# A weight unit's low part on GpSimd: four instructions of 256 columns instead of one of 1024

## What is computed

```
mem_n = rmsnorm(mem)                                  # 256 memory rows
for l in 0, 1:
    x += rmsnorm(even_mixer(x) if l == 0 else odd_mixer(x))
    x += rmsnorm(memory_cross_attention(x, mem_n @ w_mem_kv[l]))
    x += rmsnorm(relu(h @ w_ff1[l]) ** 2 @ w_ff2[l])  # 4096 wide
x = second block: conv + RWKV-7 mixer, then PEER:
    q = h2 @ peer_wq; top-16 of 128 keys twice; top-16 of the pairs
    out = sum over experts of gelu(h2 . peer_u[e]) * gate * peer_v[e]   # 16384 experts
```

## Time and profile before

| | |
|---|---|
| median of 3 runs | 3501.17 us (3498.74 to 3503.02) |
| the profiled execution | 3501.14 us |
| its span | 3499.9 us |
| PE busy | 3248.4 us (93%) |
| DVE busy | 2253.0 us (64%) |
| POOL busy | 1715.9 us (49%), of which L462 1363.0 us |
| ACT busy | 1358.3 us (39%) |
| mean granted PE clock | 0.967 |

### The profile page before, as it was taken

One profiled execution on the slowest core, in us unless ns is written; L12 is line 12 of the kernel. 1 busy time (PEld: TensorE's weight loads), 2 busy tenths in 40 slices (PEclk: granted clock), 3 DMA queues, 4 the chain that ended last, 5 costly groups with the idle time before them and its releaser, 6 DMA issues.

```text
span 3499.9 us, 48015 instructions
## 1 busy us (share of the span) xinstructions
PE 3248.4 (93%) x18529; PEld 2740.7 (78%) x18529; DVE 2253.0 (64%) x3780; ACT 1358.3 (39%) x2196; POOL 1715.9 (49%) x931
## 2 busy tenths in 40 slices
PE   6997888999899888999898898999999998999997
PEld 6886677888776677888576755799999998788886
DVE  4176646555544556553566646276998995888888
ACT  4444434222344434222253314333333674333332
POOL 6742323444332323444242202447888544888885
PEclk9998999999999999999898899999999999999999
DMA  5520212444322212443220011338899899999995
GB/s 193 183 76 25 87 58 92 137 139 139 108 91 67 84 45 88 145 144 109 69 85 31 3 37 60 120 141 292 295 325 326 266 311 304 372 357 350 354 356 219
DMA packets 304819, 584.76 MB, mean 167 GB/s; under 512 B 13520, under 2 KB 224464, under 8 KB 287312
## 3 DMA queue, kind: packets, MB, share of 16 engines
q1 hardware_dynamic: 252512, 373.32, 31.5%
q0 software_dynamic: 42576, 153.83, 12.2%
q10 hardware_dynamic: 9504, 54.53, 4.1%
HBM read 522.91 MB, written 58.72 MB: 166 GB/s over the span
## 4 chain that ended last, share of the span: by engine, by line
PE 64%; POOL 13%; DVE 9%; issue 8%; ACT 3%; DMA 1%; POOLq 0%; DVEq 0%; SPq 0%; ACTq 0%
PE bank L476 14%; PE bank L478 14%; PE bank L477 14%; POOL split_low L462 9%; PE twin L476 3%; PE twin L478 3%; PE twin L477 3%; PE bank L2854 2%; PE bank L557 2%; PE bank L2279 2%; POOL rows_arena L3220 2%; DVE branch L598 1%; POOL rows_h L3220 1%; POOL rows_near L3220 1%; DVE residual L648 1%
## 5 line engine op out<-in xcount | busy, mean ns | idle before, releaser
L462 POOL TENSOR_TENSOR split_low<-weights,split_high 128x1024 fp32r<-128x1024 f32 x554 | 1363.0, 2466 | 1494.7 <-ACT split_high L454 1490.9
L476 PE MATMUL bank<-normed_high,split_high 128*128 128x512 f32 (+1 forms) x2024 | 748.0, 370 | 34.6 <-issue 25.9
L477 PE MATMUL bank<-normed_low,split_high 128*128 128x512 f32 (+1 forms) x2024 | 736.7, 364 | 0.0
L478 PE MATMUL bank<-normed_high,split_low 128*128 128x512 f32 (+1 forms) x2024 | 736.5, 364 | 0.0
L454 ACT CAST split_high<-weights 128x1024 fp32r<-128x1024 f32 x554 | 571.4, 1046 | 359.8 <-PE bank L478 202.0
L476 PEld LDWEIGHTS bank<-normed_high,split_high 128*128 128x128 f32 x2024 | 384.1, 190 | 84.2 <-issue 37.0
L477 PEld LDWEIGHTS bank<-normed_low,split_high 128*128 128x128 f32 x2024 | 384.1, 190 | 41.6 <-issue 2.7
L478 PEld LDWEIGHTS bank<-normed_high,split_low 128*128 128x128 f32 x2024 | 383.3, 189 | 41.1
L476 PE MATMUL bank<-split_high,wide_hidden_high 128*128 128x512 f32 x768 | 300.2, 391 | 12.6 <-DVE wide_hidden_low L3076 7.4
L478 PE MATMUL bank<-split_high,wide_hidden_low 128*128 128x512 f32 x768 | 299.3, 390 | 0.0
L477 PE MATMUL bank<-split_low,wide_hidden_high 128*128 128x512 f32 x768 | 299.3, 390 | 0.0
(11 more groups left out here) (636 smaller groups left out, 6265.3 us busy)
## 6 DMA issues: line engine op xcount, KB each, us to landing
weights<-in_w_ff SPq DMA_DIRECT2D x64, 1024.0 KB, 5.5
weights<-in_peer_u SPq DMA_DIRECT2D x64, 1024.0 KB, 7.4
weights<-in_peer_v SPq DMA_DIRECT2D x64, 1024.0 KB, 8.9
weights<-in_cond_w SPq DMA_DIRECT2D x24, 1024.0 KB, 5.3
early_table<-branch SPq DMA_DIRECT2D x128, 192.0 KB, 4.4
gate_table<-arena SPq DMA_DIRECT2D x12, 2048.0 KB, 9.8
lates<-early_table ACTq DMA_DIRECT2D x32, 768.0 KB, 9.6
gates<-gate_table ACTq DMA_DIRECT2D x32, 768.0 KB, 12.5
```

Source lines behind the costliest of these rows:

```text
L462: pool.do.tensor_tensor(lo, raw_unit(u), hi.bitcast(F32), ALU.subtract).then_inc(*pool.sig("split_low", u))
L476: pe.do.matmul(o, ah, bh, start=first, stop=False)
L477: pe.do.matmul(o, ah, bl, start=False, stop=False)
L478: return pe.do.matmul(o, al, bh, start=False, stop=last)
```

## The change

`pool_split` cuts a unit along its free dimension into four pieces of 256 columns a partition and issues one subtraction for each. The wait stands ahead of the first, the semaphore is raised by the last. The result is the same, in the same tiles; the order of POOL's work and all other engines' programs are untouched. Lines after the edit move by 9: L462 becomes L471.

```
+        def unit_quarters(u):
+            n_a, width = HALF // chunks[u // 2].unit_width, chunks[u // 2].unit_width
+            if n_a >= 4:
+                return [(slice(None), slice(i * n_a // 4, (i + 1) * n_a // 4)) for i in range(4)]
+            return [(slice(None), slice(a, a + 1), slice(i, i + width // 2)) for a in range(n_a) for i in (0, width // 2)]
...
                 pool.wait_ge(at("split_high", u), unit_free(u))
-                pool.do.tensor_tensor(lo, raw_unit(u), hi.bitcast(F32), ALU.subtract
-                                      ).then_inc(*pool.sig("split_low", u))
+                rest = raw_unit(u)
+                for part in unit_quarters(u):
+                    last = pool.do.tensor_tensor(lo[part], rest[part], hi[part].bitcast(F32), ALU.subtract)
+                last.then_inc(*pool.sig("split_low", u))
```

## The result

| | before | after |
|---|---|---|
| median | 3502.1 us (3498.74 to 3504.43, 4 runs) | 3554.27 us (3550.74 to 3564.72, 4 runs) |
| span of the profiled execution | 3499.9 us | 3552.2 us |
| mean granted clock | 0.967 | 0.968 |

The account below looks back on a forecast made before the run. Bound by stage: PE in the MLP and most of PEER, POOL in the memory stage, waits for DVE at joints. Gains of 26.5 us and costs of 27.2 net +0.7 on 3501.14: 3502 us, range 3472 to 3532.

Parts of the forecast that it names:

- The price of a piece: POOL's split: three more instructions add 0.38 us a unit, between 0 and 0.54; over 554 units 210 us more POOL work.
- the first rival: POOL keeps pace: pieces join cheaply or fewer DVE passes cut in; 3487 us, down to 3475; chance 0.30.
- Point 1: Joints of stages: DVE's L598 waits for a piece, not a whole split, ending PE's waits and low clock; gain 15.5 us.
- Point 2: Even mixer, RWKV stage and last row sums: about ten other stretched DVE passes on the chain get shorter; gain 8 us.
- Point 3: End of the search: PE waits less for DVE and loses less to the lowered clock; half counted, gain 3 us.
- Point 4: Memory stage, where POOL sets the pace: some 20 of 32 units pay 0.38 us each; cost 7.5 us.
- Points 5: Stretch with two gathers a unit, where POOL is the bound: 7 units at 0.38 us; cost 2.7 us.
- 7 (3): Search: POOL's turn rises from 3.81 to 4.19 us a unit, exactly PE's pace; cost 3 us.
- 8 (1 us): First splits of a stage, on the path with their length: cost 1 us.
- Point 6: Down stage: DVE passes get in between pieces and push POOL's group past PE's, 0.6 us over 26 groups; cost 13 us.
- the second rival: POOL becomes the bound of the down stage, six of eight passes cutting in, 17.7 us a group; 3522 us, chance 0.20.
- The third rival: DVE does not get in between the pieces, POOL holding the port through all four; gains vanish, 3515 us, chance 0.15.

Follow-up runs that it names:

- middle4: Changed kernel with four pieces only from the even mixer to the RWKV stage, one instruction a unit elsewhere: 3478.94 us, ratio 0.9954 to the kernel before.
- middle8: Changed kernel with eight pieces of 128 columns in the middle stages only, whole splits elsewhere: 3475.5 us against 3500.84 for the kernel before, ratio 0.9936.

## Why the prediction was wrong

The forecast was a balance of gains and costs of 27 us each. The gains are there, 23 us; the costs were about three times as large, 75 us.

**The price of a piece** (taken: 0.38 us a unit, bounds 0 to 0.54). Four pieces after the change, with no DVE pass let in between (one stood through all four):

```profile
3161.64 2.83 POOL L471 TENSOR_TENSOR split_low<-weights,split_high 128x256 fp32r<-128x256 f32 x4
```

2.83 us against 2.405 is 0.425 a unit, 0.142 a joint, inside the bounds and near the value taken. The row decides against the 0.1 us a unit that I had estimated from the Trainium skill, "GPSIMD Engine Reference", section "Instruction dispatch", and the first rival fell with it. But the mean of all units in the trace is 3.11 us, against 2.466 before: the rest, 0.28 us, are DVE passes let in, which I had priced in the down stage only. That, on 554 units, is why POOL has 346 us more work and not 210.

**Point 1 (gain 15.5 us): right.** Before, PE waited over 3 us for L598 at three joints, one at 570, one between 900 and 965 and one between 1350 and 1430 us. From 529 to 613, 900 to 965 and 1350 to 1430 us the difference in progress falls by 6.0, 4.3 and 5.2 us, together 15.5. Close around the three waits it is 4.9, 4.0 and 5.2, together 14.1; the rest lies in smaller steps nearby, so that the sum meets the forecast to the tenth is luck. The longest L607 of this form took 1.086 us, PE no longer waits for it there, and the clock after 570 us is 1.00 where it was 0.60.

**Point 2 (gain 8 us): right.** The middle stages won 23 us in the trace of after and 21 by middle4's median; less point 1 this is 5 to 8. The largest step, 4.7 us, lies at the joint before 1721 us, where PE had waited 9.9 us for DVE's residual L648; 4.6 us are given back again by 2305 us, of which I have not followed the cause.

**Point 3 (gain 3 us) had the wrong sign.** At the end of the search PE now waits 5.1 us for DVE's L3200 where it waited 3.24, and 3.2 us are lost between 2678 and 2738 us. The last splits and gathers of the search were later, as the prediction said they might be, and DVE's last rows with them.

**Point 4 (7.5 us) measured 18.** A turn of a split and a store, which was 2.92 us:

```profile
49.07 0.58 POOL L857 DMA_DIRECT2D memory_k<-arena  x1
49.67 2.82 POOL L471 TENSOR_TENSOR split_low<-weights,split_high 128x256 fp32r<-128x256 f32 x4
52.43 0.56 POOL L857 DMA_DIRECT2D memory_k<-arena  x1
```

The turn is 3.36 us (49.07 to 52.43). Two things were too small: a unit took 2.97 us on average instead of 2.415, so 0.56 and not 0.38; and the loss fits only if not 20 of the units but all 32 were on the path, 0.56 x 32 = 18. PE needed 2.9 us for a unit and POOL's turn had been 2.92, so nothing was left with which POOL could catch up. The stretch from 33 to 135 us, which was to be 7 us longer, became 17 longer. The granted clock was 0.94 instead of 1.00 from 80 to 110 us; whether that cost anything of its own, POOL being the pace, is not told apart.

**Points 5 (2.7), 7 (3) and 8 (1 us): about right.** From 2965 to 2995 us 3.0 us were lost. From 2400 to 2700 us PE did 1702 instead of 1718 matmuls: 16 at 24 a unit are 0.67 units of 4.19 us, 2.8 us. The first splits can't be told from the rest.

**Point 6 is the step that failed: 13 us forecast, 48 measured.** The mechanism was the right one, and the count of passes that get in was not. A split and the next gather, and then DVE's passes beside them:

```profile
3156.53 3.84 POOL L471 TENSOR_TENSOR split_low<-weights,split_high 128x256 fp32r<-128x256 f32 x4
3160.53 1.09 POOL L3229 DMA_INDIRECT rows_arena<-in_peer_v_rows,own_expert  x1 [0.15 <-issue]
```

```profile
3156.59 1.17 DVE L3085 TENSOR_TENSOR wide_hidden_low<-lates,wide_hidden_high 128x384 fp32r<-128x384 f32 x1 [5.70 <-ACT wide_hidden_high L2985]
3157.68 1.09 DVE L3081 TENSOR_TENSOR lates<-lates,gates 128x384 f32<-128x384 f32 x1
3158.70 1.09 DVE L3085 TENSOR_TENSOR wide_hidden_low<-lates,wide_hidden_high 128x384 fp32r<-128x384 f32 x1
3159.71 1.08 DVE L3081 TENSOR_TENSOR lates<-lates,gates 128x384 f32<-128x384 f32 x1
3160.71 4.18 DVE L3085 TENSOR_TENSOR wide_hidden_low<-lates,wide_hidden_high 128x384 fp32r<-128x384 f32 x2
```

Three passes ended within the split, which took 3.84 instead of 2.83 us: 0.34 each. Of the 256 passes of the stage, 174 took 0.7 to 1.5 us, 5.4 of the 8 in a group; before, 8 did. The mean unit was 3.24 us, 0.41 over the undisturbed one, 1.64 a group, or 0.30 for each pass let in. So the price of a pass was right (0.3), that of the joints nearly, and the count was wrong: 5.4, not 3.5. With 1.19 us for a gather and its pauses a group takes 4 x (3.24 + 1.19) = 17.7 us (17.8 by the times at which splits end), and PE needs 16.3 (4.08 a unit before): 1.5 us a group, which is the 6.5 us per 4.3 groups of the table. I had 0.6, over 26 groups; 1.5 over the 27 groups of this window is 41 us, and the groups at either end give the rest. This is the second rival, and its 17.7 us a group, though its sum of 33 us was still short: it had six passes let in at a lower price for the joints.

Why the count was low: I took "four of eight" from the present, in which passes come in bursts, some beside a gather. A burst of passes that no longer waits 2.4 us at a time runs its whole length inside a split, one pass at each joint, as in the rows above: the change makes both the gaps and the passes that come in time for them. That is read from the timelines, and no run was made for it alone.

**The third rival (DVE shut out) was wrong** for most passes, but 19 of 256 did stand through all four pieces (below).

The range went up to 3532 because the terms that hang on one event, a DVE pass let in (points 4, 6 and 3), were priced apart. As it happened oftener than I took, they all grew together.

## What to carry to other kernels

Cut an instruction that holds a shared port only in the stages where its engine has slack and the other one is on the path; here the same edit wins 21 us in the middle stages and loses 48 in the down stage, and a table or a test by stage keeps the one without the other. Before cutting, take for each stage the pacing engine's need and the cutter's turn, then add the joints and every pass of the other engine that could now get in, up to all of them and not the share that met a gap before (5.4 of 8 got in here); where that passes the pace, each further 0.3 us is paid in full. A sum of large gains and large costs near zero is no forecast of "no change": ask for the sum stage by stage, since that is also the better kernel.

## What the runs showed of the hardware that was not expected

**A pass that starts just ahead of a run of pieces can be held through all of it.** 25 DVE passes of the changed kernel stood for over 1.2 us more than their own time. All had started while a DMA issued by POOL was ending, 24 of them in its last 0.17 to 0.5 us and one in its last 0.04, with the first piece next on POOL. The last DVE row above holds one: its second pass starts at 3161.37 us, while POOL is in the gather that ends at 3161.62, and it ends at 3164.89, just after the four pieces that begin at 3161.64. It was first, by 0.27 us, and yet took 3.5 us instead of 0.55. So did nearly all of the 25, through all four pieces, while a pass that starts during a piece waits for that piece alone. Such a start does not always mean it: of the 27 passes of L3081 and L3085 that started in the last 0.5 us of a gather with a split next, 19 were held and 8 took 0.6 to 1.4 us.

In the earlier trace rows the passes got their turn at each joint of whole splits in the same way as those that start during a piece. The rule of the exclusive lock, which the prediction took from the Trainium skill, "SBUF — State Buffer", section "SBUF: two separate sides", fits these; the held ones it does not tell. No run tries it: whether the DMA's last part or the way in which POOL starts a run of instructions makes it is open.

The wait of 8.87 us over four whole splits, on which the third rival rested, is of neither kind: it began 0.7 us after the first split, and POOL's last DMA had ended before that. Why it stood through four splits is open too. After the change the same pass at the same place got in at a joint; it and the next took 1.93 us together:

```profile
16.22 1.93 DVE L600 SCALAR_TENSOR_TENSOR mem_low<-arena,columns,mem_high 128x256 fp32r<-128x256 f32 x2 [1.17 <-ACT mem_high L595]
```

**Pieces cost POOL little by themselves, and as much again by the DVE passes that they let in.** A joint is 0.142 us, so eight pieces instead of one cost some 1 us a unit (an estimate: seven joints), and middle8 with 1750 more instructions than before lost nothing by them; a DVE pass let in costs 0.30 to 0.35 us each.
